# A hybrid decoder step: the last head's order, its output and recurrent norm inside the trunk, and the split of the mix chunks

## The chip, the cores and the metric

The kernel runs on one core of a Trainium2 chip. The metric is device time in microseconds (us) of one execution. The profile is one execution recorded by the hardware profiler; its span runs from the first to the last instruction.

## The reference, cut to what matters

One layer is computed for 1024 prompt tokens and 8 sequences of 4 new tokens (1056 token columns in all), width 1024, four attention heads and four recurrent heads:

```python
h = rms_norm(x, norm1_g)
aq, ak, av, rq, rf, ri, rg = project(h, w_in, qk_norm_g)
o_att = softmax-difference attention of two maps, per head      # diff_attn_block
f = lb + (1 - lb) * sigmoid(rf); kk = 1 - f                     # hgrn_mixer
o_rec, S = gated linear recurrence over chunks with state S     # hgrn_chunk
o_rec = rms_norm(o_rec, onorm_g) * silu(rg)                     # "recurrent norm" and gate
oa = rms_norm(o_att, subln_g) * (1 - lam_init)
x += concat(oa, o_rec) @ w_out                                  # the "mix"
x += conv_ffn(rms_norm(x, norm2_g))                             # gated MLP with a causal convolution
```

The new tokens attend to a paged cache of 256 past positions, and continue a stored recurrent state per sequence and head (`state_hgrn`), whose new value is an output (`hgrn_sample`).

## The kernel before

The program has three blocks, `prepare`, `trunk` and `tail`. At the end of a block all engines meet, and none begins the next block before the last has come; SyncE (SP) also waits there for the stores that it issued in the block (L618 on for the trunk). Within a block every engine has an order written out by hand, and semaphores tie the orders together. SP issues nearly all DMAs.

`trunk` goes over the four heads. For each it projects seven column groups of `w_in`, runs the attention over eight query blocks (`attention`), and then the recurrence (`recurrence`), mixed with the projections of the next head. The recurrence within a chunk of 128 tokens goes over levels 0 to 7: POOL takes differences of cumulated log decays, ACT exponentiates them (`level` on ACT), VectorE multiplies them with keys and queries (`weigh`), TensorE multiplies (`level` on PE), and VectorE copies the masked result into `AT` (`level_zero`, `level`). `state_updates` makes the chunk states. `outputs` multiplies the lot to the recurrent output, ACT squares it (`output_square`), VectorE gates it (`output_gate`); `output_squares`, `output_log`, `output_inverse` and `output_scale` are the recurrent norm. `attention_square`, `attention_squares`, `attention_inverse`, `attention_scale` are the same for the attention output. `sample_updates` makes the new state of the sample sequences (TensorE, then eight VectorE operations), and SP stores it (`store_states`, L540).

All the matrix products of the recurrence share two PSUM banks, `rec[0]` and `rec[1]`. Each use has a number u (`L_USE`, `SA_USE`, `O_USE`, `SR_USE`, `SU_USE`), goes to bank u % 2, and waits until the use before it on that bank has been read.

The last head has no next head to mix with. Its `last_recurrence` is mixed with the attention of the new tokens instead: for each of eight sequences TensorE turns cached keys (`turn_keys`), ACT and VectorE copy them (`keys`), then come `sample_scores`, `sample_maxima`, `sample_exponentials`, `sample_weights`, `turn_weights`, `sample_values`, `turn_outputs` and `join_maps`. In the kernel before, the last head's trunk ends with `outputs`, the squares and the gate; its recurrent norm is made at the start of `tail` (TensorE L1915, ACT L2067 and L2072, VectorE L2217).

`tail` first makes the mix. The eight chunks of the mixed width are split into a high and a low part (`part_high` on ACT, `part_low` on VectorE, order `O_ORDER`), and for 8 output blocks d and 3 token pieces n TensorE adds 24 products (`mixed`, L1882 to L1884; `mixed_first` does d = 0 to 2 of piece 0 with seven chunks first, and the last chunk, the recurrent output of the last head, after it). The split weights of blocks 0 and 1 are ready from the trunk; those of block d come from `w_out` by DMA, one ACT copy (`high(d)`, L2023) and one POOL subtraction (L1856). SP's first DMAs in the tail are the residual of piece 0 (L1818), two times two loads of stored head outputs (L1822, L1823), and then `w_out` for d = 3 to 7 (L1827). Behind the mix come the second norm and the MLP, a loop of products on TensorE to the end.

## Time and profile before

| | |
|---|---|
| median of 3 runs | 1604.2 us (1602.13 to 1604.92) |
| the profiled execution | 1599.84 us, its span 1598.1 us |
| TensorE busy over the span | 1502.4 us (94%) |
| VectorE, ACT, POOL busy | 925.6, 493.6, 507.9 us |
| mean granted TensorE clock | 0.972 |

A granted clock of 1.00 in the rows is 2.4 GHz, 0.50 is 1.2 GHz; a value between is a stretch with some of both. A share of busy time is a mean over stages with different limits, so it doesn't tell what bounds one of them.

### The profile page before, as it was taken

To read this page: it belongs to the slowest core of one execution; us is meant where nothing else is said; L and a number is where in the kernel's file an instruction comes from. 1 tells how busy PE (TensorE), PEld (TensorE's weight loads), DVE (VectorE), ACT (ScalarE), POOL (GpSimd) and SP (SyncE) were. 2 spreads that over 40 slices of the span, in tenths; PEclk is the share of its full clock that TensorE was granted. 3 is DMA by queue.
4 is the path that set the end of the run, shared out by engine and by line. 5 is a ranking of instruction groups with operands and counts; after the bars stand their busy time and mean duration, and the time that the engine had idled before them with its cause. 6 is when DMAs were issued, how large, how long until landed. Compare 5 with 4: busy or idle time off the path is not lost.

```text
span 1598.1 us, 24365 instructions
## 1 busy us (share of the span) xinstructions
PE 1502.4 (94%) x9601; PEld 1420.8 (89%) x9601; DVE 925.6 (58%) x1505; ACT 493.6 (31%) x964; POOL 507.9 (32%) x238
## 2 busy tenths in 40 slices
PE   6699899899989997879999999999999999999998
PEld 4698788798978886749999999999999999999998
DVE  5537455744574457646467475665747566474744
ACT  4446454644564455245341010101101011110111
POOL 0111221141114111313208264361725436173520
PEclk9799999999999899979999999999999999999998
DMA  5312012100310030726102020101202010120102
GB/s 196 135 54 67 14 29 83 51 27 16 95 40 27 16 94 30 227 63 199 46 15 88 32 80 27 53 26 53 66 14 79 26 53 27 53 66 27 53 0 109
DMA packets 121483, 98.16 MB, mean 61 GB/s; under 512 B 4422, under 2 KB 111175, under 8 KB 121288
## 3 DMA queue, kind: packets, MB, share of 16 engines
q1 hardware_dynamic: 119280, 88.39, 18.0%
q10 hardware_dynamic: 2136, 8.86, 1.4%
q8 instruction: 45, 0.74, 0.2%
q14 instruction: 22, 0.18, 0.0%
HBM read 77.71 MB, written 19.52 MB: 61 GB/s over the span
## 4 chain that ended last, share of the span: by engine, by line
PE 53%; DMA 1%; issue 0%; SPq 0%; ACT 0%; POOL 0%; ACTq 0%; DVE 0%
PE f_dn L1980 5%; PE f_dn L1981 5%; PE f_gp L272 5%; PE f_dn L1982 5%; PE f_up L272 5%; PE f_gp L274 5%; PE f_gp L273 5%; PE f_up L273 5%; PE f_up L274 5%; PE f_up L1882 2%; PE f_up L1883 2%; PE f_up L1884 2%; DMA m_raw<-w_out 1%; PE f_gp L2011 0%; PE f_dn L1949 0%
## 5 line engine op out<-in xcount | busy, mean ns | idle before, releaser
L264 POOL TENSOR_TENSOR m_hi<-m_raw,ones 128x1024 fp32r<-128x1024 f32 x66 | 162.5, 2462 | 446.9 <-PE f_gp L274 278.1
L272 PE MATMUL z_ps<-h_hi,w_hi 128*128 128x352 f32 x672 | 229.9, 342 | 14.6 <-DVE h_lo L295 10.2
L274 PE MATMUL z_ps<-h_hi,w_lo 128*128 128x352 f32 x672 | 220.2, 328 | 0.0
L273 PE MATMUL z_ps<-h_lo,w_hi 128*128 128x352 f32 x672 | 220.0, 327 | 0.0
L2288 DVE TENSOR_TENSOR room<-room,f_dn 128x352 f32<-128x352 f32 x264 | 137.6, 521 | 119.9 <-PE f_dn L1982 119.9
L265 POOL TENSOR_TENSOR m_lo<-m_raw,m_hi 128x1024 fp32r<-128x1024 f32 x66 | 186.0, 2818 | 5.2
L1980 PE MATMUL f_dn<-f_ahi,m_hi 128*128 128x352 f32 x528 | 172.4, 326 | 3.7 <-issue 3.7
L272 PE MATMUL f_gp<-f_hi,m_hi 128*128 128x352 f32 x528 | 172.4, 327 | 0.5 <-DVE room L2175 0.5
L634 POOL TENSOR_TENSOR w_lo<-w_raw,w_hi 128x1024 fp32r<-128x1024 f32 x28 | 66.7, 2380 | 330.3 <-ACT w_hi L1098 330.3
L1981 PE MATMUL f_dn<-f_alo,m_hi 128*128 128x352 f32 x528 | 171.0, 324 | 0.0
L1982 PE MATMUL f_dn<-f_ahi,m_lo 128*128 128x352 f32 x528 | 170.9, 324 | 0.0
L272 PE MATMUL f_up<-f_hi,m_hi 128*128 128x352 f32 x528 | 170.3, 323 | 0.0
L274 PE MATMUL f_gp<-f_hi,m_lo 128*128 128x352 f32 x528 | 169.6, 321 | 0.0
L273 PE MATMUL f_gp<-f_lo,m_hi 128*128 128x352 f32 x528 | 169.5, 321 | 0.0
L273 PE MATMUL f_up<-f_lo,m_hi 128*128 128x352 f32 x528 | 169.2, 320 | 0.0
L274 PE MATMUL f_up<-f_hi,m_lo 128*128 128x352 f32 x528 | 169.2, 320 | 0.0
L272 PEld LDWEIGHTS z_ps<-h_hi,w_hi 128*128 128x128 f32 x672 | 130.0, 194 | 17.4 <-issue 14.7
L273 PEld LDWEIGHTS z_ps<-h_lo,w_hi 128*128 128x128 f32 x672 | 130.6, 194 | 0.7
L274 PEld LDWEIGHTS z_ps<-h_hi,w_lo 128*128 128x128 f32 x672 | 129.7, 193 | 0.0
L1980 PEld LDWEIGHTS f_dn<-f_ahi,m_hi 128*128 128x128 f32 x528 | 100.1, 190 | 4.7 <-issue 4.0
L2128 ACT ACTIVATE f_cp<-f_cp 128x1056 f32<-128x1056 f32 x22 | 23.9, 1087 | 258.1 <-DVE f_cp L2267 258.1
L1981 PEld LDWEIGHTS f_dn<-f_alo,m_hi 128*128 128x128 f32 x528 | 100.2, 190 | 0.0
(303 smaller groups left out, 3054.7 us busy)
## 6 DMA issues: line engine op xcount, KB each, us to landing
w_raw<-w_in SPq DMA_DIRECT2D x28, 512.0 KB, 3.9
m_raw<-w_gate SPq DMA_DIRECT2D x22, 512.0 KB, 3.9
m_raw<-w_up SPq DMA_DIRECT2D x22, 512.0 KB, 4.0
m_raw<-w_down SPq DMA_DIRECT2D x22, 512.0 KB, 5.3
x_d<-room ACTq DMA_DIRECT2D x1, 4224.0 KB, 12.6
room<-x_d SPq DMA_DIRECT2D x3, 1408.0 KB, 7.6
room<-x_prompt SPq DMA_DIRECT2D x8, 512.0 KB, 6.5
s_kp<-cache_k SPq DMA_DIRECT2D x16, 256.0 KB, 3.0
```

The costliest lines, as they stand in the source:

```text
L264: link(nc.gpsimd.tensor_tensor(hi, raw, ones.rearrange("p (o c) -> p o c", o=1).broadcast_to(list(raw.shape)), ALU.mult))
L265: return nc.gpsimd.tensor_tensor(lo, raw, hi.bitcast(F32), ALU.subtract)
L272: nc.tensor.matmul(out, whi[:, k, :], hi[:, k, :], start=(k == 0), stop=False)
L273: nc.tensor.matmul(out, whi[:, k, :], lo[:, k, :], start=False, stop=False)
L274: last = nc.tensor.matmul(out, wlo[:, k, :], hi[:, k, :], start=False, stop=(k == chunks - 1))
L634: tt(wlo[s][:, :, :], raw[:, s, :, :], whi[s][:, :, :].bitcast(F32), ALU.subtract).then_inc(w_ready, 1)
L1882: nc.tensor.matmul(bank, ohi[d][:, k, :], hh[:, k, piece(n)], start=(first and k == chunks[0]), stop=False)
L1883: nc.tensor.matmul(bank, ohi[d][:, k, :], hl[:, k, piece(n)], start=False, stop=False)
L1980: nc.tensor.matmul(out, whi[w][:, d, :], ahi[c][:, piece(n)], start=(c == 0), stop=False)
L1981: nc.tensor.matmul(out, whi[w][:, d, :], alo[c][:, piece(n)], start=False, stop=False)
L1982: last = nc.tensor.matmul(out, wlo[w][:, d, :], ahi[c][:, piece(n)], start=False, stop=(c == G2 - 1))
L2288: v.tensor_tensor(acc[:, d, piece(n)], acc[:, d, piece(n)], dn[b][:, 0:PW], ALU.add).then_inc(dn_free[b], 1)
```

## The change

The last head gets its own bank-use numbers (`LAST_USE`), so that its uses come in a new order. On VectorE the copies of turned keys and the weighing of level 1 come ahead of `level_zero`. On TensorE, `kd2` and the rest of the last attention turn come ahead of the first turned keys; the attention squares move up behind level 6; `outputs` and the squares of the recurrent norm come around the two `sample_values`; `sample_updates` becomes the last but one. ACT does the attention norm earlier, and the logarithm and exponential of the recurrent norm at the end of the trunk; VectorE scales the recurrent output there, and makes `sample_updates` behind it. In the tail the norm is gone, and all eight chunks of piece 0 are split in one go, the first two ahead of `high(2)` and six behind it. The normalization of the sample attention output (`OS`) moves to later steps of the mix.

```diff
+LAST_USE = {"L7": 14, "SU": 20, "SA": 12, "O": 15, "SR": 17}
+def use_of(h, name):
+    return LAST_USE[name] if h == H - 1 else {"L7": L_USE[7], "SU": SU_USE, "SA": SA_USE, "O": O_USE, "SR": SR_USE}[name]
 # TensorE, last_recurrence
                     level_zero(h)
-                    turn_keys(0)
                     in_a(h, "kd2", S2, 8, 9)
                     turn_rest(h, 7)
-                    turn_keys(1)
+                    turn_keys(0)
                     pe.wait_ge(z_free, unit_of(h, RI_POS, 2) + 1)
                     in_a(h, "ri0", OR, 0, 4)
+                    turn_keys(1)
                     values(h, 7)
...
                     level(h, 6)
+                    attention_squares(h)
                     turn_weights(0), turn_weights(1)
                     level(h, 7)
                     sample_values(0)
+                    outputs(h)
+                    output_squares(h, 0)
+                    sample_values(1)
+                    output_squares(h, 1), output_squares(h, 2)
+                    turn_outputs(0)
                     sample_updates(h)
-                    sample_values(1)
-                    attention_squares(h)
-                    turn_outputs(0)
-                    outputs(h)
                     turn_outputs(1)
 # ACT, last_recurrence
                     turned(h, 7), attended(h, 6)
+                    turned_rest(h, 7)
                     keys(0), level(h, 1)
-                    turned_rest(h, 7)
                     keys(1), level(h, 2)
                     attended(h, 7)
                     keys(2), level(h, 3)
+                    attention_square(h)
...
                     sample_exponentials(1), level(h, 7)
-                    attention_square(h)
+                    attention_inverse(h)
                     output_weights(0), output_weights(1)
-                    attention_inverse(h)
                     output_square(h)
+                    for n in range(NPC):
+                        output_log(h, n)
+                    output_inverse(h)
 # VectorE, last_recurrence
-                    level_zero(h)
+                    from_a(h, "kd2", KDT, 8, 9)
                     keys(0)
                     weigh(h, 1)
-                    from_a(h, "kd2", KDT, 8, 9)
+                    from_a(h, "ri0", RI, 0, 4)
                     keys(1)
+                    level_zero(h)
                     spread_queries()
-                    from_a(h, "ri0", RI, 0, 4)
                     weigh(h, 2)
...
                     weigh(h, 6)
+                    level(h, 6)
                     sample_maxima(1)
+                    sample_weights(1)
                     weigh(h, 7)
-                    sample_weights(1)
-                    level(h, 6)
                     turned_weights(0), turned_weights(1)
+                    attention_scale(h)
                     level(h, 7)
                     sample_attended(0)
+                    output_gate(h)
+                    sample_attended(1)
+                    output_scale(h)
+                    join_maps(0)
                     sample_updates(h)
-                    sample_attended(1)
-                    join_maps(0)
-                    attention_scale(h)
-                    output_gate(h)
                     join_maps(1)
 # tail, TensorE
-                for n in range(NPC):
-                    nc.tensor.matmul(gp[n][:, 0:PW], keep["ones"][:, :], total[:, piece(n)], start=True, stop=True).then_inc(srm_ready, 1)
 # tail, ACT
-                for i in range(KC - 1):
+                for i in range(2):
                     part_high(i)
-                for n in range(NPC):
-                    act.wait_ge(srm_ready, n + 1)
-                    a(total[:, piece(n)], gp[n][:, 0:PW], ACT.Ln, ...).then_inc(sln_ready, 1)
-                (Ln and Exp of the sample norm, Exp of the three pieces)
-                part_high(KC - 1)
                 high(2)
+                for i in range(2, KC):
+                    part_high(i)
...
+                        if n == 0 and d == KC - 1:
+                            (Ln and Exp of the sample norm)
 # tail, VectorE
-                for i in range(KC - 1):
+                for i in range(KC):
                     part_low(i)
-                for n in range(NPC):
-                    dve.wait_ge(srb_ready, n + 1)
-                    v.tensor_tensor(OR[:, piece(n)], OR[:, piece(n)], total[:, piece(n)], ALU.mult).then_inc(orn_ready, 1)
-                part_low(KC - 1)
-                (scaling of OS, now at n == 1, d == 0)
```

## Rows read from the trace of the kernel before

**Rows 1.** The chain of waits, 590 to 735 us: start, length, what.

```profile
714.38 0.63 SPq L1818
...
718.58 10.36 DMA m_raw<-w_out
...
732.54 0.43 PE f_up L1882
```

**Rows 2.** Busy time by stretch: length, PE, PEld, DVE, ACT, POOL, clock, DMA share, GB/s.

```profile
690.00:697.00 7.00, 7.00 (x34) 2.67 (x33) 1.29 (x4) 0.00 (x0) 3.55 (x2) 0.50 0.00 0
713.70:717.60 3.90, 3.90 (x11) 2.69 (x12) 3.14 (x7) 3.88 (x9) 0.20 (x1) 0.60 0.40 91
...
732.00:764.00 32.00, 31.46 (x195) 31.25 (x196) 24.10 (x37) 13.16 (x28) 10.50 (x5) 1.00 0.56 164
```

**Rows 3.** VectorE in order of time, end of the trunk and start of the tail.

```profile
686.94 0.69 DVE L1449 TENSOR_TENSOR room<-room 128x512 f32<-128x512 f32 x1 [1.64 <-ACT room L1209]
...
698.59 2.16 DVE L1505 SCALAR_TENSOR_TENSOR room<-room,ends,S 128x128 f32<-128x128 f32 x8 [0.49 <-PE S L837]
...
712.97 0.41 DVE L1632 TENSOR_TENSOR OS<-OS,z_ps 128x16 f32<-128x16 f32 x4
...
721.54 1.40 DVE L2217 TENSOR_TENSOR room<-room,total 128x352 f32<-128x352 f32 x3 [4.01 <-ACT total L2072]
```

**Rows 4.** SP's waits, 600 to 760 us: waiter, releaser, us, times, longest.

```profile
SPq L516 <- PEq L516: 9.2, 1, 9.2
```

**Rows 5.** VectorE in order of time, start of the last recurrence.

```profile
644.47 1.33 DVE L1457 COPY_PREDICATED room<-lmask,S 128x512 f32<-128x512 int32 x2 [7.89 <-POOL room L669]
645.70 0.67 DVE L1601 COPY s_KT<-z_ps 128x512 f32<-128x512 f32 x1
646.30 0.81 DVE L1449 TENSOR_TENSOR room<-room 128x528 f32<-128x528 f32 x1
647.03 0.70 DVE L1450 TENSOR_TENSOR room<-room 128x528 f32<-128x528 f32 x1
...
648.45 1.49 DVE L1592 COPY s_QZ<-QS 64x32 f32<-64x32 f32 x8
```

**Rows 6.** ACT in order of time: the first level, the attention norm.

```profile
643.35 1.07 ACT L1209 ACTIVATE room<-room 128x1056 f32<-128x1056 f32 x1
...
706.17 1.26 ACT L1162 ACTIVATE room<-S,eps 128x512 f32<-128x512 f32 x2
707.46 1.28 ACT L1165 ACT_TABLE_LOAD   x1
708.75 1.06 ACT L1165 ACTIVATE room<-room 128x1024 f32<-128x1024 f32 x1
```

**Rows 7.** TensorE in order of time, last recurrence and start of the tail.

```profile
652.12 1.92 PE L888 MATMUL S<-s_KT,s_QZ 128*32 128x256 f32 x16
...
680.27 3.59 PE L888 MATMUL S<-s_KT,s_QZ 128*32 128x256 f32 x16 [0.87 <-ACT s_KT L1193]
...
689.80 1.97 PE L799 MATMUL S<-room 128*64 128x64 f32 x16
691.70 2.07 PE L907 MATMUL S<-s_VN,s_PTN 32*128 32x512 f32 x2
...
697.27 2.11 PE L837 MATMUL S<-room 32*128 32x128 f32 x16
699.22 1.02 PE L907 MATMUL S<-s_VN,s_PTN 32*128 32x512 f32 x2
...
703.14 2.52 PE L858 MATMUL S<-room,ones 128*128 128x512 f32 x4
...
707.01 0.46 PE L849 MATMUL S<-room 128*128 128x128 f32 x2 [0.91 <-ACT room L1162]
...
710.65 0.60 PE L917 MATMUL z_ps<-ident,s_OV 128*128 128x128 f32 x4
713.69 3.08 PE L1915 MATMUL f_gp<-total,ones 128*128 128x352 f32 x6 [2.44 <-PEq L516]
```

More of the change, by code:

```diff
@@ L833, in sample_updates @@
                     for half in range(2):
-                        u = SU_USE + half
+                        u = use_of(h, "SU") + half
                         bank = bank_free(h, u)
@@ L855, in attention_squares @@
                     for half in range(2):
-                        u = SA_USE + half
+                        u = use_of(h, "SA") + half
                         bank = bank_free(h, u)
@@ L860, in output_squares @@
                 def output_squares(h, n):
-                    u = SR_USE + n
+                    u = use_of(h, "SR") + n
                     pe.wait_ge(sqo_ready, 3 * h + 3)
                     bank = bank_free(h, u)
-                    mm(bank[:, 0:PW], keep["ones"][:, :], S1[:, piece(n)], start=True, stop=True).then_inc(rec_ready[u % 2], 1)
+                    mm(bank[:, 0:PW], keep["ones"][:, :], (S1 if h + 1 < H else SQ3)[:, piece(n)], start=True, stop=True).then_inc(rec_ready[u % 2], 1)
                 def turn_keys(j):
@@ L1159, in attention_inverse @@
                     for half in range(2):
-                        u = SA_USE + half
+                        u = use_of(h, "SA") + half
                         act.wait_ge(rec_ready[u % 2], rec_use(h, u))
                         a(S2[:, 512 * half:512 * half + 512], rec[u % 2], ACT.Ln, bias=keep["eps"][:, 0:1], scale=1.0 / P).then_inc(rec_free[u % 2], 1)
-                    act.wait_ge(rec_free[(SA_USE + 1) % 2], rec_use(h, SA_USE + 1))
-                    act.wait_ge(rec_free[SA_USE % 2], rec_use(h, SA_USE))
+                    for u in (use_of(h, "SA") + 1, use_of(h, "SA")):
+                        act.wait_ge(rec_free[u % 2], rec_use(h, u))
                     a(S2[:, 0:T], S2[:, 0:T], ACT.Exp, scale=-0.5).then_inc(arb_ready, 1)
@@ L1172, in output_square @@
                     for half in range(2):
-                        u = O_USE + half
+                        u = use_of(h, "O") + half
                         act.wait_ge(rec_ready[u % 2], rec_use(h, u))
@@ L1177, in output_log @@
                 def output_log(h, n):
-                    u = SR_USE + n
+                    u = use_of(h, "SR") + n
                     if n == 0:
@@ L1184, in output_inverse @@
                 def output_inverse(h):
-                    for u in (SR_USE + 1, SR_USE + 2):
+                    for u in (use_of(h, "SR") + 1, use_of(h, "SR") + 2):
                         act.wait_ge(rec_free[u % 2], rec_use(h, u))
@@ L1500, in sample_updates @@
                     for half in range(2):
-                        u = SU_USE + half
+                        u = use_of(h, "SU") + half
                         dve.wait_ge(rec_ready[u % 2], rec_use(h, u))
@@ L1516, in output_gate @@
                     for half in range(2):
-                        u = O_USE + half
+                        u = use_of(h, "O") + half
                         part = slice(512 * half, 512 * half + 512)
@@ L2054, in part_high @@
                     src, cols = part_source(n, k)
-                    if k in (H - 1, 2 * H - 1):
-                        if k == 2 * H - 1:
-                            act.wait_ge(orn_ready, n + 1)
-                    else:
+                    if k not in (H - 1, 2 * H - 1):
                         act.wait_ge(o_in[n], 32)
@@ L2083, in _ @@
                         square(n, d)
-                        if n == 1 and d == 0:
+                        if n == 0 and d == KC - 1:
+                            act.wait_ge(oms_ready, 1)
+                            a(rs[:, 1, :, :], oms[:, 0:H * NS].rearrange("p (h t) -> p h t", h=H), ACT.Ln, bias=keep["eps"][:, 0:1], scale=1.0 / P).then_inc(orb_ready, 1)
+                            act.wait_ge(orb_ready, 1)
+                            a(rs[:, 1, :, :], rs[:, 1, :, :], ACT.Exp, scale=-0.5).then_inc(orb_ready, 1)
+                        if n == 1 and d == 1:
                             act.wait_ge(on_ready, 1)
@@ L2229, in _ @@
                             sum_up(n, d)
-                        if n == 1 and d == 1:
+                        if n == 1 and d == 0:
+                            dve.wait_ge(orb_ready, 2)
+                            v.scalar_tensor_tensor(OS[:, :, :], OS[:, :, :], vector(keep, "subln_g"), rs[:, 1, :, :], ALU.mult, ALU.mult).then_inc(on_ready, 1)
+                        if n == 1 and d == 2:
                             dve.wait_ge(ohi_ready, 1)
```

25 lines of the change are left out of this document (7 added, 18 removed).

## The prediction

> **What bounds the kernel now.** I read the chain of waits first, since only what stands on it can shorten the run. Back from the end it is TensorE almost without a gap as far as 732.54 us, the first product of the mix with weight block 3. In 732 to 764 us TensorE is busy 31.46 of 32 us at a granted clock of 1.00 [rows 2], so whatever moves 732.54 moves the end by as much. Ahead of it TensorE doesn't stand on the chain: `w_out(3)` is issued by SP at 718.58, is 10.36 in flight behind the residual and the four loads that SP began to issue at 714.38, and lands at 728.94; the split on ACT and POOL takes the rest, 3.6 [rows 1]. So the tail's front is a DMA stretch: 18.85 from the first instruction of the tail, 713.69 [rows 7], to 732.54, and neither the recurrent norm nor the splitting of the chunks is in it. The chain begins with the meeting of the engines at the end of the trunk.
>
> Then I read who came last to that meeting. VectorE's last `join_maps` ends at 712.97 + 0.41 = 713.38 [rows 3]. SP had long been there: it waits 9.2 [rows 4], that is from about 704.4 on, and its last duty is the landing of the new sample states. Their last update ends at 698.59 + 2.16 = 700.75 [rows 3], so the store costs 3.65 from there to SP's arrival, hidden behind 9 us of other work.
>
> So the change is worth what it does to two things: the time at which the trunk ends, SP's stores included, and the state in which TensorE meets 732.54. All steps below are in times of this profiled execution.
>
> **Step 1, the norm leaves the tail: nothing.** Gone are three products (3.08 for the three [rows 7]), logarithms and exponentials on ACT, and VectorE's scaling, 1.40 [rows 3]. All of it is over 6 us before `w_out(3)` lands. SP's orders up to that load are the same, so the 18.85 stay. If this cover were gone, up to 6 us would be to gain; nothing in the change starts these loads earlier in the tail. The sample norm that moves to the middle of the mix is a few short ACT and VectorE instructions on engines busy 13.16 and 24.10 of 32 [rows 2]; nothing as well.
>
> **Step 2, the start of the last recurrence: 1.5 earlier.** VectorE idles 7.89 ahead of `level_zero`, for POOL's clearing of `AT` [rows 5]. The work put ahead doesn't fill all of it, since weighing needs ACT's exponentials of level 1. They end at 643.35 + 1.07 = 644.4 [rows 6], and now come behind `turned_rest` and the first keys: about 645.0, an estimate. From there VectorE has the weighing (0.81 and 0.70, 1.35 as they overlap, by the starts), `ri0` and `keys(1)` (0.6 each, a full bank copy is 0.67), `level_zero` (1.23 from its start to the next) and the eight copies of `spread_queries`, 1.49 [rows 5]: 650.3. `sample_scores(0)`, which waits for these copies, starts at 650.4 in place of 652.12 [rows 7]: 1.7. Its sixteen large products take 1.92, but 3.59 at another place, 680.27 [rows 7], where the clock was low; if the new pauses on TensorE ahead of it have that effect, the gain is none. Bounds 0 and 1.7; I take 1.5, since each new pause is under 2 us by these times, and the one of 2.44 [rows 7] is the shortest that my rows show the clock to fall behind. From there to the scores of the last sequences the order of PE, ACT and VectorE stays, and VectorE or PE is nearly always occupied, so the shift is carried along.
>
> **Step 3, level 6 ahead of the second maxima: 0.4 later.** VectorE now waits for TensorE's level 6 and copies it (0.7 and 0.7, estimates: one copy of `level_zero` is half of 1.33 [rows 5]) before the maxima on which ACT, VectorE and TensorE hang in turn. Level 7 on TensorE in its turn now needs the bank that ACT frees with the first attention logarithm: a table load, 1.28, and half of 1.26 [rows 6], together 1.9, behind the exponentials of level 7. In the old order the same stretch held the last weighing, the weights and their turn, 686.94 to 689.80 [rows 3, 7], 2.86. 1.4 + 1.9 - 2.86 = +0.44. Level 7 starts at 689.80 - 1.5 + 0.45 = 688.75.
>
> **Step 4, the end of the trunk: 4.5 later.** From level 7 on, with old durations by starts [rows 7]: level 7 1.9 (to 690.65), `sample_values(0)` 5.57 (696.2), `outputs` 3.64 (707.01 to 710.65; 699.85), ACT's square of the last half 0.6 (700.5, half of the 1.06 of a full width [rows 6], with overhead), one square of the norm 0.7 (between 1.03, a third of 3.08 at a clock of 0.60, and half of that; 701.2), `sample_values(1)` 3.3 (it took 3.92, 699.22 to 703.14, and half of 5.57 is the lower bound; 704.5), two more squares 1.4 (705.9). Then, one behind the other and with no cover: logarithm 0.5, table load 1.28 and exponential 1.06 [rows 6], scaling 1.3 (the three pieces took 1.40 [rows 3]), `join_maps(0)` 0.85 (two groups of 0.41 [rows 3]): 710.9. Now VectorE makes `sample_updates`, 2.16 [rows 3]: 713.1. Only then can SP issue the store, and the 3.65 that 9 us of work hid are bare: 716.8. `join_maps(1)`, some 0.85, lies under it. Against 713.38 that is +3.4; that sum already contains steps 2 and 3 (-1.5, +0.45), so the new end of head alone is +4.5.
>
> The Trainium skill, "ScalarE: Activation LUTs", section "What ACT_TABLE_LOAD costs", gives each switch of the table a drain of about 1.38 behind the 1.28 of the load. Here the load at 707.46 is followed by its exponential at 708.75, 1.29 later [rows 6], so no drain shows. By the page the two loads on the path would add 2.8; by the rows they don't, and the sum goes by the rows.
>
> **Step 5, TensorE's clock at the start of the mix: 1.5 later.** With nothing of the norm to wait for, the first three blocks, 72 products of about 0.16 (195 in 31.46 us [rows 2]), 11.6 in all, are done some 13 to 15 after the start of the tail. TensorE then pauses 4 to 6 until 18.85. In the old run the third block came late and ended just ahead of it. A pause of 2.44 at the meeting was followed by 3.9 us at a mean clock of 0.60 [rows 2, 7], that is about 3.1 us at 1.2 GHz and 1.55 us of work lost. The same loss now falls on the stretch that sets the end. Bounds: 0, if the clock holds, and 3.5, if it stays at 0.50 for 7 us as in 690 to 697 [rows 2]. I take 1.5.
>
> The Trainium skill says the same of such pauses ("TensorE: Matmul & The Clock Gate", section "Why this matters for your kernels"): a gap between bursts of matmuls brings the half clock back. It speaks against this change; the price above is the trace's.
>
> **Sum.** 3.4 + 1.5 = 4.9 over 1599.84, the profiled execution's own time: 1604.7. The median of the runs stands 4.4 above that execution, so I add 4.9 to 1604.2: 1609.1.
>
> **The rivals.**
> First, not slower: TensorE runs at 2.4 GHz to the end of the trunk. `sample_values(0)` and its neighbours ran at 0.50 in 690 to 697 [rows 2], behind a long pause that the attention squares now partly fill. At full clock `sample_values(0)` takes 2.8 less, the second 0.5 less, and the last scores (3.59 against 1.92) 1.7 less. The store would land at 716.8 - 5.0 = 711.8, `join_maps(1)` at about 709: the trunk ends 1.6 earlier, and with step 5 the sum is -0.1, 1604.1; without step 5, -1.6, 1602.6. It decides once 3.4 us of the 5.0 are had. For it: the pause ahead of level 7 shrinks from two to one. Against: the work there is the same small and part-array products that ran at 0.50 although TensorE was busy all 7 us.
>
> Second, slower still: `outputs` falls into a low stretch. It costs 3.64 more, `sample_values(1)` 2.3 more, the squares 1.0 more: 4.9 + 6.9 = 11.8, 1616.0. For it: the 7 us at 0.50 directly ahead of it; against: the clock was back by 698 in the old run, on the products behind `sample_values(0)`.
>
> Third, the page's drain on the two loads of the path, 2.8 more: 1611.9. The load row speaks against it.
>
> Fourth, faster: the landing of `w_out(3)` isn't what the tail waits for, and mixing starts as soon as its splits are done. Then 4 to 6 come back, step 5 falls away, and 3.4 - 5 gives 1602.6. Against: the 10.36 of the load stand on the chain themselves [rows 1].
>
> **How the numbers follow.** A difference under 0.2%, 3.2 us, is what measurement of this kernel can't tell from none. Forecast 0.55, with its own range from 1605.5 to 1613; first rival 0.25, second 0.10, third 0.05, fourth 0.05. The forecast is a sum of terms whose bounds reach 1.6 below (step 2 and `sample_values` at their favourable ends, no step 5) to 12 above. The range 1602 to 1615 leaves out most of the second rival and the lowest part of the first. Faster: a third of the first rival and half of the fourth, 0.11. Same: the rest of those two and the lower fifth of the forecast, 0.30. Slower: 0.59.
>
> **What would show it.** In the changed profile SP should be last to the meeting, its wait there on the landing of the sample states, about 3.6 behind VectorE's last update; the first instruction of the tail stands at 716 to 718. `w_out(3)` should still be about 15 behind that and the product with block 3 about 18.9. TensorE should pause 4 to 6 ahead of it and show a clock well under 1.00 behind it. `sample_scores(0)` should start near 650.4. If the trunk ends before 713.4, or the product with block 3 follows its start by much less than 18.9, the prediction is wrong.

## The result and the profile after

The changed kernel is slower: 1609.06 us, median of 22 runs (1600.57 to 1612.97), against 1602.74 for 22 runs of the kernel before (1597.38 to 1610.08). The ratio is 1.0033, 95% interval 1.0021 to 1.0045, so 5.3 us, from 3.4 to 7.2; the 6.3 between the two medians lies inside that. The profiled execution took 1606.53, with a span of 1604.7 at a mean granted clock of 0.972; that of before took 1599.84.

Two profiled executions can't simply be laid over each other. VectorE's last combining of the attention, work that the change doesn't touch and that comes before all that it does, ends at 636.57 in the profile of before, at 635.84 in that of after, and between 633.27 and 642.38 over all profiles of this study. So I measure from that end, the anchor, in every profile: "+14.61" means 14.61 us behind it. From there to the end of the span it is 961.53 in before, 968.86 in after, and 966.42 in a second profile of the changed kernel: 7.3 and 4.9 longer, around the 5.3 of the times.

First the chain of waits of after, from the end of the trunk on (start, length, what), which answers to [rows 1].

```profile
721.23 0.63 SPq L1835
725.26 10.56 DMA m_raw<-w_out
735.85 1.07 ACT m_hi L2036
736.99 2.40 POOL m_lo L1873
739.43 0.43 PE f_up L1899
```

It is the same chain, later: the first issue of the tail, the load of `w_out(3)`, its splits, the product with block 3. From the first issue to that product it is 18.20; in before it was 18.16 [rows 1]. SP's waits between 600 and 760 us (waiter, releaser, us, times, longest) answer to [rows 4], its issues in order of time follow.

```profile
SPq L634 <- DMA hgrn_sample<-room: 2.8, 1, 2.8
SPq L528 <- PEq L528: 0.2, 1, 0.2
```

```profile
716.64 0.40 SPq L552 DMA_DIRECT2D hgrn_sample<-room  x1
721.23 0.63 SPq L1835 DMA_DIRECT2D room<-x_d  x1
```

The 9.2 that SP waited for the other engines are 0.2 now: SP is last, and what held it is the landing of the sample states. VectorE shows why, in order of time (answers to [rows 3, 5]).

```profile
644.39 1.56 DVE L1466 TENSOR_TENSOR room<-room 128x528 f32<-128x528 f32 x1 [1.35 <-ACT room L1223]
...
648.91 1.48 DVE L1609 COPY s_QZ<-QS 64x32 f32<-64x32 f32 x8
...
712.51 1.26 DVE L1543 TENSOR_TENSOR room<-room 128x1056 f32<-128x1056 f32 x1 [3.70 <-ACT room L1201]
...
714.46 2.15 DVE L1522 SCALAR_TENSOR_TENSOR room<-room,ends,S 128x128 f32<-128x128 f32 x8
```

The updates of the sample states (714.46) stand behind the scaling (712.51), which stands behind 3.70 of waiting for ACT's inverse root. They end at 716.61, SP issues the store at 716.64, and its next issue comes 4.6 later. In before the same updates ended at 700.75 [rows 3], 13.6 ahead of the first issue of the tail.

TensorE in order of time (answers to [rows 7]):

```profile
647.92 1.06 PE L887 MATMUL z_ps<-ident,s_kp 128*128 128x128 f32 x8 [1.88 <-DVE s_KT L1618]
650.45 3.63 PE L900 MATMUL S<-s_KT,s_QZ 128*32 128x256 f32 x16 [1.47 <-DVE s_QZ L1609]
662.35 3.34 PE L830 MATMUL S<-room 128*128 128x128 f32 x16 [1.77 <-DVE room L1484]
...
692.58 1.16 PE L811 MATMUL S<-room 128*64 128x64 f32 x16 [1.69 <-ACT room L1176]
...
695.67 3.64 PE L923 MATMUL S<-s_V,s_PT 128*32 128x512 f32 x16
699.24 0.80 PE L861 MATMUL S<-room 128*128 128x128 f32 x2
...
720.88 0.79 PE L1932 MATMUL f_dn<-f_rs,ones 128*128 128x128 f32 x2 [8.45 <-ACT f_rs L2072]
739.43 0.43 PE L1899 MATMUL f_up<-f_hi,m_hi 128*128 128x352 f32 x1 [0.54 <-POOL m_lo L1873]
```

Two things there weren't in the forecast. `sample_scores(0)`, the products at 650.45, take 3.63; they took 1.92 [rows 7]. And the pause ahead of block 3 is 0.54, since TensorE comes to the mix after 8.45 of idleness and does its first blocks slowly. The stretches (length, then PE, PEld, DVE, ACT and POOL busy, granted clock, DMA share, GB/s; answers to [rows 2]) give the clock of both:

```profile
644.00:650.40 6.40, 3.10 (x27) 2.71 (x25) 5.91 (x14) 3.52 (x6) 1.38 (x2) 0.90 0.85 247
650.40:656.00 5.60, 5.55 (x40) 3.49 (x41) 2.71 (x6) 1.10 (x2) 0.00 (x0) 0.50 0.82 274
656.00:662.30 6.30, 4.58 (x45) 4.40 (x44) 5.03 (x9) 1.54 (x2) 4.05 (x4) 1.00 0.79 239
662.30:666.00 3.70, 3.65 (x18) 3.26 (x20) 3.27 (x8) 0.00 (x0) 0.63 (x1) 0.57 0.27 79
...
720.50:724.50 4.00, 2.89 (x8) 2.17 (x8) 2.50 (x3) 3.98 (x10) 2.08 (x2) 0.50 0.40 112
724.50:728.00 3.50, 2.57 (x9) 2.58 (x10) 3.05 (x6) 0.36 (x1) 0.49 (x1) 0.50 1.06 383
728.00:732.00 4.00, 4.00 (x18) 4.00 (x17) 0.00 (x0) 0.00 (x0) 0.00 (x0) 0.62 1.07 375
732.00:736.00 4.00, 4.00 (x26) 4.00 (x25) 0.00 (x0) 0.15 (x1) 0.00 (x0) 1.00 1.17 307
736.00:740.00 4.00, 3.46 (x22) 3.17 (x21) 1.96 (x3) 3.07 (x6) 2.39 (x1) 1.00 0.67 162
```

TensorE is at 2.4 GHz (1.00) while it waits and computes by turns in 656 to 662 and at the end of 732 to 740, but at 1.2 GHz (0.50) behind the pauses of 1.88 and 1.47 near 650, and for some 10 us behind the 8.45 at the meeting: the starts of its products are 0.29 apart up to 730.9 and 0.16 from then on, which is the 0.62 of 728 to 732.

The milestones of all profiles, in us behind the anchor:

| kernel | scores(0) start (length) | level 7 | updates end | first issue of the tail | block 3 | end of span |
|---|---|---|---|---|---|---|
| before | 15.55 (1.92) | 53.23 | 64.18 | 77.81 | 95.97 | 961.53 |
| after | 14.61 (3.63) | 56.74 | 80.77 | 85.39 | 103.59 | 968.86 |
| after, second profile | 14.61 (3.50) | 53.97 | 78.02 | 82.64 | 100.84 | 966.42 |
| 1: updates before scaling | 14.59 (3.63) | 56.67 | 77.30 | 81.92 | 99.94 | 965.20 |
| 2: old front | 15.54 (1.92) | 53.54 | 77.55 | 82.16 | 100.60 | 965.15 |
| 3: new front alone | 14.60 (3.43) | 53.31 | 65.72 | 80.08 | 98.47 | 963.10 |
| 3, second profile | 14.60 (3.38) | 53.30 | 65.71 | 80.03 | 98.66 | 963.28 |
| 4: weights first | 14.60 (3.63) | 56.66 | 80.68 | 85.38 | 102.64 | 968.35 |
| 5: norm back in the tail | 14.61 (3.39) | 53.96 | 71.86 | 76.47 | 94.95 | 959.46 |
| 6: 1 and 2 together | 15.52 (1.92) | 53.54 | 74.14 | 78.76 | 96.84 | 961.31 |
| 7: before, weights first | 16.16 (1.92) | 53.50 | 64.86 | 76.92 | 91.68 | 957.13 |
| 8: best of all | 15.68 (1.92) | 53.67 | 64.26 | 73.54 | 88.29 | 952.68 |
| 9: pauses filled | 14.58 (1.92) | 53.93 | 77.97 | 82.59 | 102.11 | 968.90 |

From block 3 to the end it is 865.56 in before, 865.27 and 865.58 in the two of after: all of the loss lies ahead of block 3, as the first paragraph of the prediction has it. Over all profiles of the table this last stretch takes 864.39 to 866.79, so a difference of 1 us between two ends says little by itself; the column of block 3 is the safer one.

### The profile page after: what moved, and what is told of

It is laid out like the page before. It is cut to its first block, busy times and chain, and to the rows that moved or that the text cites. A ratio compares the mean times of both kernels' runs of the same rounds, so it can differ in the third digit from the quotient of the medians.

```text
span 1604.7 us, 24368 instructions
## 1 busy us (share of the span) xinstructions
PE 1501.7 (94%) x9601; PEld 1421.7 (89%) x9601; DVE 936.9 (58%) x1503; ACT 496.6 (31%) x964; POOL 509.9 (32%) x238
## 4 chain that ended last, share of the span: by engine, by line
PE 53%; DMA 1%; issue 0%; SPq 0%; ACT 0%; POOL 0%; ACTq 0%; DVE 0%
PE f_dn L1993 5%; PE f_dn L1994 5%; PE f_gp L272 5%; PE f_dn L1995 5%; PE f_up L272 5%; PE f_gp L274 5%; PE f_gp L273 5%; PE f_up L273 5%; PE f_up L274 5%; PE f_up L1899 2%; PE f_up L1900 2%; PE f_up L1901 2%; DMA m_raw<-w_out 1%; PE f_gp L2024 0%; PE f_dn L1962 0%
## 5 line engine op out<-in xcount | busy, mean ns | idle before, releaser
L1995 PEld LDWEIGHTS f_dn<-f_ahi,m_lo 128*128 128x128 f32 x528 | 100.3, 190 | 0.0
```

What stands on the lines that cost most here:

```text
L1995: last = nc.tensor.matmul(out, wlo[w][:, d, :], ahi[c][:, piece(n)], start=False, stop=(c == G2 - 1))
```

## The experiments

My theory behind the result: the loss is made in two places. The store of the sample states is bare at the end of the trunk (step 4), and the new front doesn't pay, as its pauses put `sample_scores(0)` at 1.2 GHz (step 2 with its sign turned). Rivals: the norm in the trunk costs by itself, through ACT's tables; or the tail is what got longer. Ratios are to the kernel before on the same chip.

**1, the updates ahead of the scaling (on the changed kernel, VectorE).**

```diff
                     output_gate(h)
+                    sample_updates(h)
                     output_scale(h)
                     join_maps(0)
-                    sample_updates(h)
                     join_maps(1)
```

> The changed kernel, with one move on VectorE: sample_updates comes ahead of output_scale, in the pause of 3.7 us in which VectorE waits for ACT's exponential. If the bare store is what ended the trunk late (first theory), the last update ends some 3.6 us earlier, at about 713 in place of 716.6, the store lands at 716.8 and the tail starts near 717, 3 to 4 us earlier; the time falls by as much against the changed kernel (about 1605.5 where that has 1609). If the low clock in the last recurrence is the whole loss (second theory), the tail's start moves by under 1 us.

Ratio 1.0003 (0.9989 to 1.0018), 1605.66. VectorE and SP in order of time:

```profile
716.24 2.16 DVE L1522 SCALAR_TENSOR_TENSOR room<-room,ends,S 128x128 f32<-128x128 f32 x8 [2.25 <-PE S L849]
718.31 1.25 DVE L1543 TENSOR_TENSOR room<-room 128x1056 f32<-128x1056 f32 x1
```

```profile
718.42 0.40 SPq L552 DMA_DIRECT2D hgrn_sample<-room  x1
723.02 0.63 SPq L1835 DMA_DIRECT2D room<-x_d  x1
```

The updates end 3.47 earlier behind the anchor, and the tail starts 3.47 earlier; from the issue of the store to the next one it is 4.60 as before the edit. Scaling and joining now lie under the landing. By the profile the span is 3.7 shorter than the first of after; in time 0.30% of the 0.33% that were lost come back, 4.8 us, give or take 3 by the two intervals, which don't touch. The order of these VectorE steps alone makes about half of the loss by the profiles (3.5 of 7.3, in two executions where the state updates fall to half clock, as told below) and most of it by the times: the store theory holds.

**2, the old front on the changed kernel.** TensorE, ACT and VectorE get the order of before as far as `values(h, 7)`; the end of the head stays as changed.

```diff
@@ TensorE @@
+                    turn_keys(0)
                     in_a(h, "kd2", S2, 8, 9)
                     turn_rest(h, 7)
-                    turn_keys(0)
+                    turn_keys(1)
...
-                    turn_keys(1)
@@ VectorE @@
+                    level_zero(h)
...
-                    level_zero(h)
```

> The changed kernel with the start of the last recurrence (level zero, first keys, first weighing, kd2, ri0) in the old order on TensorE, ACT and VectorE. Second theory (the new pauses on TensorE ahead of sample_scores(0) bring the low clock, and the shift is carried to the end): the scores take 1.9 instead of 3.6, the last scores start 2 to 3 us earlier against the first row of the stretch, and the trunk ends 2 to 3.3 us earlier. First theory alone, with step 2 as predicted: the start of the scores gets later by 0.8 and the trunk's end by 0 to 1.5.

Ratio 1.0029 (1.0015 to 1.0043), 1606.84. TensorE in order of time:

```profile
654.69 1.92 PE L900 MATMUL S<-s_KT,s_QZ 128*32 128x256 f32 x16
```

The scores start 0.93 later than in the new front and are back at 1.92, the state updates at 2.02; level 7 starts at +53.54, 3.2 earlier than in the first profile of after and 0.4 earlier than in the second. The span is 3.7 or 1.3 shorter than theirs, but 3.0 or 0.2 at block 3. The times don't tell it from the changed kernel: the intervals lie on each other.

**3, the new front alone, on the kernel before.** Exactly the moves of the front that the change makes, nothing else.

```diff
@@ VectorE @@
-                    level_zero(h)
...
+                    from_a(h, "kd2", KDT, 8, 9)
+                    from_a(h, "ri0", RI, 0, 4)
+                    level_zero(h)
```

> The kernel before with only the new start of the last recurrence. By step 2 of the prediction 1.5 us faster (bounds 0 and 1.7). If the clock goes low in the scores as in the profile of the changed kernel, 1 to 3 us slower; TensorE's granted clock in the 4 us behind the start of sample_scores(0) tells which.

> The kernel before with only the new start of the last recurrence, once more: in its first profile the scores were slow but state_updates was not, and level 7 stood at 53.3, as before. If that is chance, level 7 comes near 56.7 in some executions; if the order behind it matters, at 53.3 again.

Ratio 0.9990 (0.9971 to 1.0008), 1601.71; the execution of the second profile took 1600.04. TensorE in that second profile:

```profile
649.62 3.38 PE L888 MATMUL S<-s_KT,s_QZ 128*32 128x256 f32 x16 [1.48 <-DVE s_QZ L1592]
```

The scores start 0.95 earlier and take 1.5 more, in both profiles; the state updates take 2.02 as in before; the next scores start 0.5 later than in before (+27.36 and +27.31 against +26.79). At level 7 both stand where before stood (+53.31 and +53.30 against +53.23): the gain of 1.5 that step 2 took isn't there, and nothing is lost either. The tail's first issue is 2.3 and 2.2 later all the same, and the span 1.6 and 1.75 longer. That arises behind level 7, where this kernel has no edit: the products of `sample_updates` take 3.78 in both profiles, 2.11 in before and 2.51 in experiment 7, whose trunk is that of before. Whether this belongs to the new front isn't shown. By the times there is neither gain nor loss that this measurement can tell: the interval goes from 4.6 faster to 1.3 slower, so it doesn't exclude a gain of 1.5 by itself.

**The changed kernel again**, one more profile, for the size of that effect.

> The changed kernel once more, for a second profile: whether the low clock in sample_scores(0) and state_updates (level 7 at 56.7 from the last combining, 53.2 in the kernel before) is the same in another execution, or whether level 7 comes anywhere between 53.5 and 57.

1610.64. TensorE:

```profile
656.99 3.50 PE L900 MATMUL S<-s_KT,s_QZ 128*32 128x256 f32 x16 [1.48 <-DVE s_QZ L1609]
...
667.87 2.02 PE L830 MATMUL S<-room 128*128 128x128 f32 x16 [1.77 <-DVE room L1484]
```

The scores are slow again, but the state updates behind them aren't, as in the two profiles of experiment 3, and level 7 is at +53.97 in place of +56.74. So the fall at the scores belongs to the new order (it is in every profile of it, 3.38 to 3.63), and the second one at the state updates, 1.3 on its instruction and 2.8 at level 7, comes in some executions only. The pause right ahead of them is 1.77 in both. What does go with it lies ahead of all that the change moves. In the eight profiles of the new front, experiment 9 among them, TensorE has a low stretch just behind the anchor. Where the granted clock is 0.50 to 0.52 in the first 3 us and 0.99 or 1.00 in the next 3, the state updates are slow (this kernel's first profile, experiments 1, 4 and 9); where it is 0.59 to 0.63 and then 0.80 to 0.84, they aren't (its second profile, both of experiment 3, experiment 5). Both kinds occur with the old front too (0.53 and then 1.00 in before, 0.59 and 0.84 in experiment 7), where the state updates take 2.02 in all five profiles. So it goes with the new front and that kind of execution together; how the one leads to the other isn't shown.

**4, the weight loads first (on the changed kernel, SP in the tail).**

```diff
+                for d in range(3, 5):
+                    output_weights(d)
                 residual(0)
...
-                for d in range(3, KC):
+                for d in range(5, KC):
                     output_weights(d)
```

> The changed kernel with w_out(3) and w_out(4) issued ahead of the residual and the stored head outputs at the start of the tail. If the landing of w_out(3) alone sets the tail's front (the prediction's reading), it lands about 4 us behind its issue and the product with block 3 follows as soon as the first three blocks are done, 13 to 18 us behind the start of the tail in place of 19: 1 to 5 us faster than the changed kernel. If TensorE, at its low clock after the meeting, is as late as the load, the gain is 0.5 us or less.

Ratio 1.0011 (0.9992 to 1.0030), 1605.63. Two stretches of its tail:

```profile
719.00:727.00 8.00, 6.25 (x19) 5.53 (x20) 6.78 (x8) 5.89 (x13) 4.63 (x3) 0.50 0.83 245
727.00:731.00 4.00, 4.00 (x20) 4.00 (x20) 0.96 (x1) 0.00 (x0) 0.57 (x1) 0.72 1.06 377
```

Block 3 no longer waits for anything, but comes only 0.95 earlier (17.26 behind the first issue): behind the long idle of the meeting TensorE stands at 0.50 for the first 8 us of its tail, and its three blocks take as long as the load did. The profile is 0.5 shorter than after's first; the times, 3.5 shorter with intervals that overlap, leave it between nothing and some 7 us.

**5, the norm back in the tail.** The changed kernel's front, level 6, early attention norm and `outputs`, without the norm's squares, logarithms, inverse and scaling in the trunk; the tail is that of before. The updates come when `sample_values(1)` is done.

```diff
@@ TensorE, from outputs(h) on @@
-                    output_squares(h, 0)
                     sample_values(1)
-                    output_squares(h, 1), output_squares(h, 2)
                     turn_outputs(0)
                     sample_updates(h)
                     turn_outputs(1)
```

> The changed kernel's trunk without its recurrent norm, with the tail of the kernel before, which makes the norm there; sample_updates takes the two bank uses that the squares of the norm had. Step 1 of the prediction (the norm in the tail is hidden under the landing of w_out(3)): the tail from its first instruction to the product with block 3 takes 18.9 as in both kernels, and the trunk, without logarithms, table load, exponential and scaling ahead of the store, ends about 6 us earlier than in the changed kernel: 5 to 7 us faster than it. Rival: the norm costs its 4 to 6 us in the tail, and the time stays that of the changed kernel.

Ratio 0.9990 (0.9972 to 1.0009), 1598.05. VectorE's updates:

```profile
704.04 2.16 DVE L1517 SCALAR_TENSOR_TENSOR room<-room,ends,S 128x128 f32<-128x128 f32 x8 [0.24 <-PE S L849]
```

They end at +71.86, 8.9 earlier than in the first profile of after. Of these, 2.8 lie ahead of level 7, since the state updates weren't slow here (+53.96 against +56.74); from level 7 to the end of the updates it is 17.90 where both profiles of after have 24.03 and 24.05. So the norm, put ahead of the store, cost 6.1, and by the two ratios 0.43%, 6.9 us, come back, with intervals that don't touch. The tail takes 18.48 from its first issue to block 3 (18.20 in after, 18.16 in before). Its chain of waits runs through the norm and the split of block 2, not through the load; POOL's split of block 3 and the first product with it follow:

```profile
717.44 1.28 ACT total L2084 x3
...
720.34 2.35 POOL m_lo L1868
722.73 0.43 PE f_up L1894
```

```profile
726.84 2.40 POOL L1868 TENSOR_TENSOR m_lo<-m_raw,m_hi 128x1024 fp32r<-128x1024 f32 x1 [4.17 <-ACT m_hi L2035]
...
729.29 0.43 PE L1894 MATMUL f_up<-f_hi,m_hi 128*128 128x352 f32 x1
```

The split of block 3, which hangs on the load, ends at 729.24, and the product comes 0.05 later, without a wait of its own. The norm in the tail is still covered, but only just: it holds up the third block through `high(2)`, and TensorE, behind a pause of 2.07 ahead of 722.73, runs at a clock of 0.61 up to 727. In before the third block was done 1.19 ahead of the split; in the two profiles of experiment 3 the product came 0.38 and 0.05 behind it. So the norm cost at most 0.4 where it was, and 6 us where it was put. The rest of the change gains 2.1 by the profile, nothing that the times can tell.

**6, experiments 1 and 2 together.**

> The changed kernel with the old start of the last recurrence and with sample_updates ahead of output_scale on VectorE. If the two losses are separate and add up, the product with block 3 comes 3.65 and 3.0 earlier, 6.6 in all, against the last combining of attention, and 1 us later than in the kernel before (ratio 1.0006). If the low clock comes back elsewhere when one of them is gone, less than 5 us of the 7.6 come back.

Ratio 0.9989 (0.9972 to 1.0006), 1599.47, and by the profile 961.31 behind the anchor, 0.2 from before. The two edits add: 3.7 and 3.7 by the profiles alone, 7.5 together, against the first profile of after, where the state updates fell to half clock; against the second it is 5.1 together. With both undone nothing is left of the change that the times can tell.

**7, the weight loads first, on the kernel before.** SP as in experiment 4, and ACT makes the high part of block 2 behind the first two parts of the residual, ahead of the norm.

```diff
@@ ACT @@
-                for i in range(KC - 1):
+                for i in range(2):
+                    part_high(i)
+                high(2)
+                for i in range(2, KC - 1):
                     part_high(i)
...
                 part_high(KC - 1)
-                high(2)
```

> The kernel before with two moves at the start of its tail: SP issues w_out(3) and w_out(4) ahead of the residual and the stored outputs, and ACT makes high(2) behind the first two splits. If the loads' order is what holds the product with block 3 (first theory), it comes 15 to 16 us behind the start of the tail in place of 18.85, 3 to 3.5 us earlier, and TensorE has no pause ahead of it. If TensorE's own work at the start of the mix is as late, 1 us or less.

Ratio 0.9982 (0.9964 to 1.0000), 1598.17. POOL's split of block 3 in order of time, and a stretch of the tail:

```profile
720.58 2.40 POOL L1858 TENSOR_TENSOR m_lo<-m_raw,m_hi 128x1024 fp32r<-128x1024 f32 x1 [6.70 <-ACT m_hi L2025]
```

```profile
714.30:718.30 4.00, 3.98 (x25) 3.98 (x26) 1.78 (x5) 3.96 (x8) 0.00 (x0) 1.00 1.04 321
```

The split is done at 722.98, and the product with block 3 follows at 724.95, when TensorE has done the three blocks before it. That is 14.76 behind the first issue in place of 18.16: 3.4 earlier. The span is 4.4 shorter by the profile, but 0.9 of this lies ahead of the edit (the tail starts at +76.92 against +77.81 behind the same trunk), and the time is at the edge of what can be told. The cover that step 1 named is taken away here. TensorE goes through its blocks at a granted clock of 1.00; in experiment 4, where it is at 0.50, the same order of the loads gave 0.95. The load of block 5 is now the one that decides: in the chain of waits of this profile it is 11.47 in flight from 718.53 on, and TensorE waits 0.72 for its split.

**8, the best of all.** The old front; the attention norm early as in the change; `sample_updates` between the two `sample_values`, ahead of `outputs`; no recurrent norm in the trunk; the tail of experiment 7.

```diff
@@ TensorE @@
                     sample_values(0)
+                    sample_updates(h)
                     outputs(h)
-                    output_squares(h, 0)
                     sample_values(1)
-                    output_squares(h, 1), output_squares(h, 2)
                     turn_outputs(0)
-                    sample_updates(h)
                     turn_outputs(1)
```

> What the runs point to: the old start of the last recurrence, the attention norm moved up as in the change, sample_updates between the two sample_values ahead of outputs (so that its store lands under other work), the recurrent norm in the tail, and the tail with w_out(3), w_out(4) and high(2) first. The trunk should end 4 to 5 us earlier than in the kernel before, the product with block 3 come another 3 us earlier: 7 to 8 us faster than before (ratio 0.995). If the meeting of the engines is then set by ACT or TensorE, or if the clock falls in the mix, 3 to 5 us.

Ratio 0.9936 (0.9913 to 0.9960), 1591.44: 0.64% or 10.2 us faster than before, and by the two ratios 0.97% or some 15 us faster than the changed kernel. VectorE, and SP's waits:

```profile
699.72 2.16 DVE L1517 SCALAR_TENSOR_TENSOR room<-room,ends,S 128x128 f32<-128x128 f32 x8 [0.59 <-PE S L849]
...
709.66 0.41 DVE L1644 TENSOR_TENSOR OS<-OS,z_ps 128x16 f32<-128x16 f32 x4
```

```profile
SPq L528 <- PEq L528: 4.1, 1, 4.1
SPq L634 <- DMA hgrn_sample<-room: 3.5, 1, 3.5
```

The updates end at 701.88, the store's landing is waited for 3.5, and then SP waits 4.1 for the others: the store is covered again, and VectorE's last `join_maps`, done at 710.07, is last to the meeting, as in before. The tail begins 4.3 earlier than there (+73.54 against +77.81), and block 3 comes 14.75 behind it, as in experiment 7. Which of the moves in the trunk bring the 4.3 isn't told apart.

**9, the pauses of the new front filled (on the changed kernel).** TensorE makes three more products of 128x128x512 whose result nobody reads; they add work and change no output.

```diff
                     values(h, 7)
+                    for _ in range(2):
+                        mm(Sg[1], ident[:, :], S2[:, 0:512], start=True, stop=True)
                     turn_keys(2)
+                    mm(Sg[1], ident[:, :], S2[:, 0:512], start=True, stop=True)
                     sample_scores(0)
```

> The changed kernel with three more matrix products (128x128 by 128x512, into a bank that is free then, result unused) on TensorE in the pauses ahead of sample_scores(0): two ahead of turn_keys(2), one behind it. If the pauses are what brings the clock of 1.2 GHz into the scores, they take 1.9 in place of 3.6, state_updates 2.0 in place of 3.3, and level 7 comes 2 to 3 us earlier against the last combining. If the low clock there has another cause, the scores stay at 3.6 and level 7 comes at the same place or up to 1 us later.

Ratio 1.0011 (0.9995 to 1.0028), 1601.24. TensorE, and two stretches:

```profile
647.79 1.88 PE L1037 MATMUL S<-room,ident 128*128 128x512 f32 x4
...
652.38 1.92 PE L900 MATMUL S<-s_KT,s_QZ 128*32 128x256 f32 x16 [0.62 <-DVE s_QZ L1612]
...
661.68 3.46 PE L830 MATMUL S<-room 128*128 128x128 f32 x16 [1.78 <-DVE room L1487]
...
739.91 0.66 PE L1902 MATMUL f_up<-f_hi,m_hi 128*128 128x352 f32 x1 [2.28 <-POOL m_lo L1876]
```

```profile
652.30:656.00 3.70, 3.62 (x46) 2.77 (x47) 3.16 (x8) 1.12 (x2) 0.00 (x0) 1.00 1.06 345
...
739.90:744.00 4.10, 4.09 (x16) 4.09 (x17) 4.10 (x5) 1.10 (x3) 2.57 (x1) 0.60 0.48 142
```

With the pauses filled the scores take 1.92 at 1.00: the pauses are what slowed them. It doesn't make the new front pay in this profile. The state updates fell to 3.46, and in the tail the load of block 3 was 11.98 in flight (10.56 in after), so a pause of 2.28 came ahead of the product, which then starts at a slow 0.66. Behind it the clock is 0.60 for 4.1 us, where after has 1.00; from there to the end it is 866.79, 1.2 to 1.5 more than in the two profiles of after. That is the mechanism of step 5, at the price that it put on it, in an execution where a pause did come, if a shorter one. By the times this kernel is 3.5 us faster than the changed one, with intervals that overlap, and the profiled execution (1608.46) is the second slowest of its twelve.

## Why the prediction was right, and where it wasn't

The forecast of 4.9 later met 5.3 by the times, with 7.3 and 4.9 in the two profiles. Its sum is right, though two of its terms are not. That 1609.06 lies so close to 1609.1 is luck: the 4.9 were added to the median of three runs, 1604.2, and the 22 runs of before have 1602.74. Of the signs that the prediction named, SP is last to the meeting, its wait there is on the sample states, and block 3 follows the start of the tail as late as before. The pause of 4 to 6 ahead of it and the low clock behind it didn't come, and the trunk ends later than the 3.4 of step 4: the tail's first issue is 7.6 and 4.8 later than in before.

**Step 1, nothing: right.** From the first issue of the tail to block 3 it is 18.20 where it was 18.16, and experiment 5 shows the norm in the tail covered. The cover is thinner than the 6 us that the step counted, though. The step measured the norm against the landing of the load; what hangs on the norm is `high(2)`, the split of block 2 and the third block of products, and they were done 1.19 ahead of block 3 in before, and level with it in experiment 5.

**Step 2, 1.5 earlier: wrong.** Of the 1.7 by which the scores should start earlier 0.94 came: the first weighing multiply took 1.56 in place of 0.81 [rows 5] (1.35 in the second profile), so the eight copies of the queries end 14.55 behind the anchor and not 13.7. The rows tell what that multiply ends with: POOL's second subtraction of a level, which runs at +8.39 to +9.54 in after. In all thirteen profiles the multiply ends 0.55 to 0.58 behind the end of that subtraction, whether it starts 0.24 to 0.26 ahead of that end, as in the old front, or 0.77 to 1.06, as in the new. So its earlier start was worth nothing. No run moved the POOL instruction, so that it holds the multiply is an alignment and not a tested cause. And the products took 3.63 and 3.50 for 1.92, which is the lower bound that the step named, 1.7 earlier less 1.7 slower; with 0.94 in place of 1.7 it is a loss, of 0.8 and 0.6. I took the other end. "Each new pause is under 2 us by these times" was true (1.88 and 1.47), and the conclusion from it wrong: that the shortest pause in my rows with a fall behind it was 2.44 didn't mean that shorter ones have none. Experiments 3 and 9 show it from both sides. Measured to the last scores, the step is +3.26 in one profile and +0.65 in the other; the difference is the second low stretch, at the state updates (0.57 in 662.3 to 666), whose cause stays open. In experiment 3, with neither that stretch nor the other changes, it is +0.08 at level 7: the gain was used up, no more.

The Trainium skill ("TensorE: Matmul & The Clock Gate", section "Why this matters for your kernels") warns of long gaps between bursts of matmuls. The 8.45 at the meeting agrees, with 0.50 behind it. The pauses of 1.88 and 1.47 are shorter than the gap that it warns of, and the granted clock behind them is 0.50 all the same.

**Step 3, 0.45 later: right** in size, +0.25 and +0.09 from the last scores to level 7, where these scores were 0.40 and 0.71 shorter than in before; experiment 2, whose last scores take 3.58 as in before, has +0.32.

**Step 4, 4.45 later: right.** From level 7 to the first issue of the tail it is 28.65 and 28.67 against 24.58 in before, +4.1. Within it, 24.03 from level 7 to the end of the updates (24.35 forecast), and 3.6 for the bare store, if the 1.0 from the end of the meeting to the first issue [rows 1, 3] is taken off the 4.62. Experiment 1 takes 3.5 of it back.

**Step 5, 1.5 later: wrong in this kernel.** The pause of 4 to 6 was 0.54 and 0.32. "13 to 15 after the start of the tail" for the first three blocks took no account of the clock after an 8.45 idle at the meeting: it is 0.50 until about 730.9, so they take 18.0, hidden under the load, and the clock is at 1.00 again in time for block 3. The low stretch came earlier than I put it, where it costs nothing. Experiment 9 shows the price where the pause does come, 1.2 to 1.5.

At block 3 the measured steps add up to 7.6 in the first profile and 4.9 in the second. A term of -1.5 that was +3.26 or +0.65 and one of +1.5 that was 0 make up for each other within 0.7 in the second profile only. That the sum is right is luck in these two terms; step 4 is the mechanism that the runs bear out, with the small steps 1 and 3.

**The rivals.** The first, 2.4 GHz to the trunk's end, didn't happen: the products at 695.67 take 3.64, as in before (693.70). The second came in a small part: `outputs` runs from 699.24 to 703.60 at a mean clock of 0.87, 0.7 longer than the 3.64 forecast and not twice as long; as level 7 took 1.1 in place of 1.9, it ends 11.0 behind level 7's start where 11.1 was forecast. The fourth falls with the chain of waits and experiment 7: the load does decide, though in the changed kernel by 0.54 only, and putting it first there (experiment 4) gave 0.95 and not 4 to 6. The third is told by ACT in order of time:

```profile
710.10 1.28 ACT L1201 ACT_TABLE_LOAD   x1
711.39 1.08 ACT L1201 ACTIVATE room<-room 128x1056 f32<-128x1056 f32 x1
```

The exponential starts 1.29 after the load of the table did. The drain behind each load that the Trainium skill states ("ScalarE: Activation LUTs", section "What ACT_TABLE_LOAD costs") doesn't show here either.

**What stays open.** How much the front costs in the changed kernel: 0.2 to 3.0 at block 3 by pairs of profiles (experiment 2), less than the times can tell. By the times experiments 1 and 3, which both have the new front, aren't told from before, so the profiles may overstate it. Whether POOL is what holds the first weighing multiply, how the clock behind the anchor leads to that of the state updates, and why `sample_updates` is slow in experiment 3, wasn't tried.

## What to carry to other kernels

Before moving work out of one place, look at what is free there because of something longer beside it: the norm lay under a load of 10 us, and in the trunk it came to lie ahead of a store on which all engines wait. Let the stores that a meeting of the engines waits for be issued first, and put the work that nobody waits for behind them; here that one order was worth 3.5 us by the profiles and 4.8 by the times. A kernel with the store covered, the norm back in the tail and the loads that decide the next stage issued first was 10 us faster than the one before and some 15 faster than the changed one. An earlier start on TensorE is worth only what is left after the pauses that it opens: count them, and price what follows at half clock.

## What the runs showed of the hardware

- Pauses of 1.88 and 1.47 us, 1.06 of work between them, were followed by products at a granted clock of 0.50 in after. All seven profiles of the new front have such pauses, of 1.65 to 1.94 and 1.47 to 1.49, and slow products behind them (3.38 to 3.63 for the 1.92 at 1.00). With the pauses filled by unused products they took 1.92.
- An idle of 8.45 us was followed by some 10 us at 0.50 (720.9 to 730.9), although TensorE had work for most of it. An idle of 2.44 at the same meeting was followed by 0.60 over 3.9 us in before, and by 1.00 in experiment 7.
- A VectorE multiply that started beside a POOL subtraction ended 0.55 to 0.58 us behind it in all thirteen profiles, and took 0.81 to 1.63 by how early it had started; its second half, without one beside it, took 0.69 to 0.71.
- The same work, upstream of every change, ended at times up to 9.1 us apart (633.27 to 642.38) in different executions, more than the effect under study. Measured from a milestone late in that common part, two profiles of one kernel agreed within 0.2 us (experiment 3) where their spans differed by 2; of the changed kernel they differed by 2.4 all the same, and the trunk of before, run again in experiment 7, ended 0.9 earlier behind the anchor.
